# Cross attention with the state-space copy ahead of the exponential, and more places for expert weights

## The reference

```python
# block one
x = x + mixed @ w_out                    # convolution and dilated attention
x = x + memory_cross_attention(rms_norm(x), rms_norm(mem), w_xq, w_xk, w_xv, w_xo)
x = x + hierarchical_moe(rms_norm(x), ..., w1, w3, w2)        # stage one: 32 experts, ff 512
x = rms_norm(x)
# block two
x = x + mixed2 @ w_out_2                 # forgetting attention and a state-space layer
x = x + _hier_moe(rms_norm(x), ..., w_gate, w_up, w_down)     # stage two: 32 experts, ff 256
```

## Time and profile before

| | |
|---|---|
| median of 3 runs | 1988.65 us (1988.5 to 1989.75) |
| profiled execution, its own time | 1994.36 us |
| its span | 1992.5 us, 19337 instructions |
| TensorE busy | 1680.9 us (84%) |
| VectorE, ScalarE, GpSimd busy | 507.1, 332.1, 325.3 us |
| DMA | 437.02 MB, mean 219 GB/s |
| chain that ended last | TensorE 59%, DMA 28%, VectorE 5% |
| largest DMA parts of it | w1/w3/w2 into ring 17%, stage two's up weights into ring 10% |

### The profile page before, as it was taken

How to read it: one execution, slowest core, us unless ns; L and a number is a source line. 1 busy time by engine, 2 the same in 40 slices (tenths; PEclk the granted TensorE clock), 3 DMA queues, 4 the chain that set the end, 5 groups by cost and what they waited for, 6 DMA issues and landing times.

```text
span 1992.5 us, 19337 instructions
## 1 busy us (share of the span) xinstructions
PE 1680.9 (84%) x7362; PEld 846.6 (42%) x7362; DVE 507.1 (25%) x1204; ACT 332.1 (17%) x735; POOL 325.3 (16%) x325
## 2 busy tenths in 40 slices
PE   3999998899779787777777758899999997887775
PEld 2445776444444432322222224645744444543432
DVE  2466666120223320100000011622501015311110
ACT  2001552120222000000000021222510003011111
POOL 0011002956010111111111110011001010122212
PEclk9999999899899798999999988999999998899888
DMA  9112103420453599999999956761012235899994
GB/s 278 63 43 85 64 1 127 168 95 23 169 201 134 191 414 417 414 417 412 413 402 403 404 186 221 188 173 43 1 42 85 85 132 216 316 399 403 402 389 155
DMA packets 101675, 437.02 MB, mean 219 GB/s; under 512 B 15608, under 2 KB 23448, under 8 KB 75344
## 3 DMA queue, kind: packets, MB, share of 16 engines
q1 hardware_dynamic: 58320, 295.03, 38.9%
q10 hardware_dynamic: 24800, 109.99, 13.5%
q0 software_dynamic: 18464, 30.76, 6.1%
HBM read 414.19 MB, written 40.91 MB: 228 GB/s over the span
## 4 chain that ended last, share of the span: by engine, by line
PE 59%; DMA 28%; DVE 5%; ACT 2%; POOL 2%; issue 2%; SPq 1%; ACTq 0%; DVEq 0%; POOLq 0%
PE ps L245 28%; DMA ring<-in_w 17%; PE ps L1607 10%; DMA ring<-in_w_expert_up 10%; PE ps L1199 7%; PE ps L2078 2%; PE ps L1623 1%; PE ps L655 1%; PE ps L663 1%; DMA ring<-in_positions 1%; PE ps L2116 1%; PE ps L1225 1%; PE ps L452 1%; PE ps L2425 1%; PE ps L1008 1%
## 5 line engine op out<-in xcount | busy, mean ns | idle before, releaser
L1607 PE MATMUL ps<-ring,work 128*64 128x256 f32 (+1 forms) x2112 | 395.2, 532 | 118.4 <-DMA ring<-in_w 71.2
L1607 PEld LDWEIGHTS ps<-ring,work 128*64 128x64 f32 x2112 | 162.8, 151 | 357.3 <-issue 172.2
L245 PE MATMUL ps<-hT,ring 128*128 128x512 f32 x640 | 280.7, 598 | 2.5 <-DVE hT L1254 1.3
L1623 PE MATMUL ps<-ring,work 128*64 128x512 f32 x784 | 183.2, 601 | 38.3 <-issue 36.4
L245 PEld LDWEIGHTS ps<-hT,ring 128*128 128x128 f32 x640 | 122.2, 192 | 156.6 <-issue 154.0
L1725 DVE TENSOR_TENSOR work<-work,ps 128x256 f32<-128x256 f32 (+1 forms) x64 | 22.7, 355 | 644.5 <-ACT work L1684 625.4
L245 PE MATMUL ps<-ring,hT 128*128 128x512 f32 (+1 forms) x320 | 124.7, 550 | 0.3 <-PE ps L245 0.3
L1771 POOL DMA_INDIRECT hres<-work,rowdst x33 | 51.7, 1566 | 442.9 <-ACT work L1694 442.6
L245 PE MATMUL ps<-work,ring 128*128 128x128 f32 (+2 forms) x800 | 117.5, 293 | 1.7 <-DVEq L229 0.6
L1199 PE MATMUL ps<-ring,hT 128*128 128x512 f32 x256 | 112.9, 595 | 1.9 <-DVEq L229 0.9
L245 PEld LDWEIGHTS ps<-work,ring 128*128 128x128 f32 x800 | 105.6, 191 | 8.1 <-DVE ring L2482 2.3
(11 more groups left out here) (425 smaller groups left out, 1642.6 us busy)
## 6 DMA issues: line engine op xcount, KB each, us to landing
ring<-in_w SPq DMA_DIRECT2D x66, 2048.0 KB, 16.8
ring<-in_w ACTq DMA_DIRECT2D x30, 2048.0 KB, 20.5
ring<-in_w_expert_gate SPq DMA_DIRECT2D x34, 1024.0 KB, 19.9
ring<-in_w_expert_up SPq DMA_DIRECT2D x34, 1024.0 KB, 29.4
ring<-in_w_expert_down ACTq DMA_DIRECT2D x28, 1024.0 KB, 21.6
ring<-in_w_in SPq DMA_DIRECT2D x13, 2048.0 KB, 15.2
ring<-in_w_out SPq DMA_DIRECT2D x4, 2048.0 KB, 7.7
ring<-in_w_expert_down SPq DMA_DIRECT2D x6, 1024.0 KB, 14.4
```

The lines of the kernel that those rows point to most:

```text
L245: last = nc.tensor.matmul(out_, l, r, start=i == 0, stop=i == len(pairs) - 1)
L1607: last = nc.tensor.matmul(ps[64 * hf:64 * hf + 64, bank, 0:ff].rearrange("p (w n) -> p w n", w=2), xT[:, k, :], up[:, :, k * ff + hf * hw: ...
L1623: last = nc.tensor.matmul(ps[64 * hf:64 * hf + 64, bank, :], hT_[:, i % nch, 64 * (i // nch):64 * (i // nch) + 64], down[:, i, hf * 512:hf ...
```

## The change

In `xattn_act` the copy of state-space block i-1 is put ahead of the exponential of round i. The tiles `x`, `hT` and `xn` become three parts of one tile `kept`. A stage of experts may use it as a further place: a third in stage one (up weights over `hT` and `xn`, down weights over `x`), and two more in stage two, six in all. SP issues the loads for these places as soon as the first gathered block has landed (`xg6_0`), those that overwrite `x` also after its stores (`xinit6`). The planner's scratch moves from `hT` to the route area `RT` and to `junk`. Six more semaphores are used twice, which the tensor engine clears between the blocks. The calls of the stage functions pass 3 and 6 in place of 2 and 4, and the lag of the down products is told from `ff`, so it stays.

```diff
-        x = sb("x", [P, T, D])
-        hT = sb("hT", [P, KD, SEQ])
-        xn = sb("xn", [P, T, D])
+        kept = sb("kept", [P, 3 * T * D])
+        x = kept[:, 0:T * D].rearrange("p (t n) -> p t n", t=T)
+        hT = kept[:, T * D:2 * T * D].rearrange("p (k n) -> p k n", k=KD)
+        xn = kept[:, 2 * T * D:3 * T * D].rearrange("p (t n) -> p t n", t=T)
...
             for i in range(NX + 2):
+                if 1 <= i <= NX:
+                    s5_turned_act(act, i - 1)
                 if i < NX:
                     act.wait_ge(S("x5_max"), i + 1)
                     if i >= 2:
                         act.wait_ge(S("x5_turned"), since("x5_turned") + i - 1)
                     nc.scalar.activation(pr(i)[:, 0:MEM], ps[:, i % 2, 0:MEM], ACT.Exp, bias=nmax[:, i:i + 1], scale=-1.0,
                                          accum_out=den[:, i:i + 1]).then_inc(S("x5_probs"), 1)
-                if 1 <= i <= NX:
-                    s5_turned_act(act, i - 1)
...
-        late_rank = hl(256, T, NE)
-        egate = hl(384, 8, NE)
+        late_rank = hl(RT, 0, T, NE)
+        egate = hl(RT, 128, 8, NE)
...
-        Ab = hl(1672, 8, SLOT)
-        be_f = hl(2200, NOV, NE)
+        Ab = hl(junk, 0, 8, SLOT)
+        be_f = hl(junk, 512, NOV, NE)
...
-            if places == 2:
-                up, down = (ring[:, 0:2, :], ring[:, 2, :]) if e % 2 == 0 else (ring[:, 4:6, :], ring[:, 3, :])
+            place = e % places
+            if places == 3 and place < 2:
+                up, down = (ring[:, 4:6, :], ring[:, 3, :]) if place else (ring[:, 0:2, :], ring[:, 2, :])
             else:
...
+                size = 3 * KD * ff
+                in_ring = places * 2 // 3
+                if place < in_ring:
+                    at = (place + 2) % in_ring * size
+                    wv = ring[:, :, :].rearrange("p a n -> p (a n)")[:, at:at + size]
+                    up, down = wv[:, 0:2 * KD * ff], wv[:, 2 * KD * ff:size]
+                else:
+                    at = (places - 1 - place) * size
+                    up, down = kept[:, at + size - 2 * KD * ff:at + size], kept[:, at:at + size - 2 * KD * ff]
...
+            sp.wait_ge(S(f"xg{m}_0"), since(f"xg{m}_0") + 16)
+            for e in range(places * 2 // 3, places):
+                load_up(e)
+                if places == 3:
+                    sp.wait_ge(S(f"xinit{m}"), since(f"xinit{m}") + 16 * T)
+                load_down(e)
+                if e == 4:
+                    sp.wait_ge(S(f"xinit{m}"), since(f"xinit{m}") + 16 * T)
             for e in range(places, NE):
                 sp.wait_ge(S(f"up{m}"), since(f"up{m}") + e - places + 1)
                 load_up(e)
```

More of the change, by code:

```diff
@@ L133, in shared_semaphores @@
         shared[f"xg9_{q}"] = (f"xg6_{q}", 16 * NE // 2 // 4)
-    for i in range(4):
-        shared[f"w9_{i}"] = (f"w6_{i}", (16 if i % 2 else 32) * NE // 2)
+    for i in range(6):
+        shared[f"w9_{i}"] = (f"w6_{i}", (16 if i % 2 else 32) * len(range(i // 2, NE, 3)))
     for slot in range(RING):
@@ L1412, in slots_dve @@
                 dve.wait_ge(S(f"ranks{m}"), since(f"ranks{m}") + t1)
-                late = hl(0, T, 2, NE)
+                late = hl(junk, 0, T, 2, NE)
                 rank = (ps[:, 7, 0:3 * NE] if t0 == 0 else ps[:, 4, 0:NE]).rearrange("p (t e) -> p t e", t=n)
@@ L1450, in hl @@
             return v
-        late_rank = hl(256, T, NE)
-        egate = hl(384, 8, NE)
-        cnt = hl(640, 8, NE)
-        over = hl(896, NE, SEQ // SLOT - 1)
-        dests = hl(1120, 8, 4)
-        Gb = hl(1152, 8, NOV + 1)
-        Bb = hl(1288, 8, NOV)
-        Rb = hl(1416, 8, 2 * NOV)
-        Ab = hl(1672, 8, SLOT)
-        be_f = hl(2200, NOV, NE)
-        te = hl(2712, T, NE)
+        late_rank = hl(RT, 0, T, NE)
+        egate = hl(RT, 128, 8, NE)
+        cnt = hl(RT, 384, 8, NE)
+        Bb = hl(RT, 640, 8, NOV)
+        over = hl(RT, 1024, NE, SEQ // SLOT - 1)
+        Gb = hl(RT, 1248, 8, NOV + 1)
+        Rb = hl(RT, 1408, 8, 2 * NOV)
+        te = hl(RT, 1664, T, NE)
+        dests = hl(RT, 1792, 8, 4)
+        Ab = hl(junk, 0, 8, SLOT)
+        be_f = hl(junk, 512, NOV, NE)
         def late_dve(m, piece):
@@ L1507, in late_dve @@
                 L(dve.tensor_tensor(te, te, row("first_row").unsqueeze(1).to_broadcast(full), ALU.add))
-                pick = hl(0, T, 2, NE)
+                pick = hl(junk, 0, T, 2, NE)
                 L(dve.tensor_tensor(pick, E12[:, :, :, :], te.unsqueeze(2).to_broadcast([P, T, 2, NE]), ALU.mult))
@@ L1579, in expert_views @@
         def expert_views(ff, places, e):
[L1581 to L1588 removed]
+            place = e % places
+            if places == 3 and place < 2:
+                up, down = (ring[:, 4:6, :], ring[:, 3, :]) if place else (ring[:, 0:2, :], ring[:, 2, :])
+            else:
+                size = 3 * KD * ff
[7 more added lines that the diff above has]
+                    up, down = kept[:, at + size - 2 * KD * ff:at + size], kept[:, at:at + size - 2 * KD * ff]
+                up = up.rearrange("p (w n) -> p w n", w=2)
             return up, down.rearrange("p (c n) -> p c n", n=D)
@@ L1629, in moe_pe @@
         def moe_pe(pe, m, ff, places):
-            lag = 1 if places == 2 else 2
+            lag = 1 if ff == FF1 else 2
             n = lambda what, v: pe.wait_ge(S(f"{what}{m}"), since(f"{what}{m}") + v)
@@ L2610, in _ @@
             ranks_pe(6)
[L2611 to L2612 removed]
+            moe_pe(pe, 6, FF1, 3)
+            over_pe(pe, 6, FF1, 3)
             pe.wait_ge(S("pool_over"), 1)
@@ L2624, in _ @@
             ranks_pe(9)
-            moe_pe(pe, 9, FF2, 4)
-            over_pe(pe, 9, FF2, 4)
+            moe_pe(pe, 9, FF2, 6)
+            over_pe(pe, 9, FF2, 6)
         @block.scalar
```

31 lines of the change are left out of this document (12 added, 19 removed).

## The result

| | before | changed |
|---|---|---|
| median | 1988.58 us (1987.36 to 1989.75, 4 runs) | 1966.96 us (1964.34 to 1970.19, 4 runs) |
| ratio to before, 95% interval | | 0.9892 [0.9872, 0.9912] |
| profiled execution, its span | 1994.36, 1992.5 us | 1970.19, 1968.4 us |

The change gains 21.6 us, not 36, and the time lies 1 us above the range. The direction was right. The span of the profiled execution became 24.1 us shorter (these executions lie 5.8 and 3.2 us above the medians), and reading both traces at the same instructions splits these 24.1 us. Each column is the time from the event of the column before to this one, the first from the span's start; "up 31" are the up products of expert 31, "last down" the last down products of a stage, each by its start.

What follows compares the result with a forecast made beforehand. Transfers were taken to set 749 us of the expert stages, and ScalarE's copy to hold up TensorE in the cross attention. 14.5 + 10 + 11.5 = 36 us off the 1988.65 us median gave 1952.6 us, range 1942 to 1966.

Steps and rivals of the forecast that it cites:

- Cross attention, 14.5 forecast: Cross attention with ScalarE's copy ahead of the exponential: 2.8 + 8.4 + 3.3 = 14.5 us gained, bounds 9 and 21.8.
- The two groups of four rounds: Cross attention between value products: period 12.1 us in place of 16.3, 4.2 us gained, twice.
- the first piece: Start of the cross attention: copy 2 held until the first block store lands near 519.5 us; 2.8 us gained.
- nothing holds copy 2: Rival, cross attention: the first store lands before 514 us; 19.6 + 21.5 = 41 us gained, 1947.5 us; chance 0.10.
- Stage one, 10 forecast: Third place in stage one: 12.7 earlier start - 5.3 down transfer + 3.3 = 10.7, taken as 10 us; bounds 5 and 13.
- that lost 3.3 us, which a deeper queue fills: End of stage one: DMA share 0.62 over the last 8.65 us before the last up load landed; 3.3 us regained.
- Stage two, 11.5 forecast: Two more places in stage two: 9.0 + 3.8, less half the last down transfer, taken as 11.5 us; bounds 4 and 15.
- here all of it is paid back: Stage two: the 5.3 us of downs ahead of ups is regained, as the two overflow blocks' loads close the stream.
- the head start that goes into downs and isn't paid back: Rival, both expert stages: new places fill with downs first, TensorE late at the end; 23.5 us gained, 1965 us; chance 0.18.
- The stream itself runs slower: Rival, expert stages: a 4.8% lower rate over 749 us loses the 36 us; at 6%, 1998 us; chance 0.03.
- VectorE binds every round: Rival, cross attention: VectorE or the blocks' stores bind; 9 us there, total 30.5, 1958 us; chance 0.11.
- the new place does nothing: Rival, expert stages: the new place's loads wait as late as the first products; only cross attention counts, 1974 us; chance 0.03.

Runs made afterwards that it cites:

- late_first_load: The changed kernel, with SP issuing the first expert's up weights after the cross attention: 1959.41 us, ratio 0.9846; repeated in another set, 1952.92 us.
- down_late: The changed kernel, with down weights issued only two experts ahead in stage one and four in stage two, as before the change: 1968.26 us, ratio 0.9905.
- swap_only: The kernel before, with only ScalarE's copy of the state-space block put ahead of the exponential: 1977.17 us, ratio 0.9943.

## Why the prediction was wrong

**Cross attention, 14.5 forecast, 11.7 measured.** The two groups of four rounds gave 8.1 (forecast 8.4), the last piece 3.3 (3.3). The step that failed is the first piece, "1.8 us there and 1.0 in the fourth round: 2.8". It gave 0.3: the value products came at 529.10, and at 529.43 before. The mechanism was right, as late_first_load shows; three things were mis-sized. The store landed at 520.5 and not 519.5, since the issue 1.6 us earlier brought it nothing, and TensorE's clock stayed at half up to 526.4, because the engine stood still for 7.5 us. And the sum takes every round at full clock, where the kernel before had half of it from 512.1 to 524.8 us. That is luck of the execution: from the first scores to the first value products the traces with the old order take 23.0 us twice and, where the clock came back sooner, 20.8 twice, against 22.7 in the changed kernel. Measured by the shorter ones the first piece lost 1.9 us. In late_first_load the first value products begin 13.0 us after the first scores, in the changed kernel 22.7 us, so the hold and its clock cost 9.7 us; the rival "nothing holds copy 2" priced them at 5.1.

The Trainium skill ("DMA: Bandwidth & Descriptors", Queues, rings and completion order) says that each DMA engine goes round its queues a packet at a time. The traces agree in that the store had no right of way: in the kernel before it landed at 520.47 us and the load beside it at 520.29, and it took 10.0 us in the changed kernel and no store more than 5.8 with the load moved. That the small store ends only with the load, which the prediction drew from that rule, the page doesn't state; it is what these traces show.

**Stage one, 10 forecast, 7.0 measured.** The loads are issued 12.7 us earlier, and with the downs held back (down_late) the stretch shrinks by 12.7 against the kernel before and by 10.5 and 11.8 against the other two profiles with two places. The down transfer ahead of the ups cost 3.0 to 4.5 (forecast 5.3). What failed is "that lost 3.3 us, which a deeper queue fills": with the third place the share before the last landing is 0.36. A place more doesn't put work behind the last up weights, since the stage has no more to load (this reason is read from the program; the ten profiles with three places all have the low share). Another 1.2 went behind them, to the clock: the last up products took 9.94 us (8.78 in the earlier trace rows), and 7.09 in other runs.

**Stage two, 11.5 forecast, 2.4 measured.** Here the largest part is lost, and the step is "here all of it is paid back". I took the overflow blocks' loads for what closes the stage, because the queue had 3.8 us of empty time around them. But in the kernel before TensorE waits only 0.15 us for the last of them, in its timeline:

```profile
1964.24 3.67 PE L1607 MATMUL ps<-ring,work 128*64 128x256 f32 x32 [1.50 <-DVE work L1880]
1968.07 3.67 PE L1607 MATMUL ps<-ring,work 128*64 128x256 f32 x32 [0.15 <-DMA ring<-in_w_expert_up]
```

From expert 31's up products on, TensorE's own work sets the end there, so only their start counts, and it came 6.1 us sooner. With the downs held back it was 11.2: 9.0 of earlier start and 2.2 more, which I put down to the queue's empty time before expert 31's weights (a share of 0.78 over the 5.4 us before their landing in the kernel before); the missing 5.2 goes to the downs ahead of the ups and, as that run can't tell them apart, to SP's long issues (last section). This split is worked out and not tested by itself. The row with the wait of 0.15 us stands in the trace of the kernel before, and the prediction doesn't use it. Then came the wait for the gathered rows, which I had nowhere: the rows are gathered only after expert 28's result, and TensorE, which waits less for weights, now comes to them before the 9.2 us of the gather are over.

**The rival that held** is the head start that goes into downs and isn't paid back: stage one 5, stage two 4, 1965 us. It was given 0.18, and the row above and the fact that a stage can't fill its own end would have made it the likeliest. Its 1965 is near the 1966.96 partly by chance: the first piece of the cross attention is 2.5 lower than it has it, and the stretch between the stages gave 3.3 that belong to no part.

**Not foreseen:** the 3.3 us between the stages. Over the thirteen profiles that stretch has 521.5 to 522.6 us eight times and 525.0 to 525.6 five times, in one kernel both. In all five long ones the first 64 products take 9.77 to 9.91 us, in all eight short ones 7.13: that is 2.7 of the 3 to 4 us. The length comes by chance, and 3 to 4 us of it can stand in any difference between two profiles. The six further semaphores that TensorE clears there cost nothing that shows: swap_only, without them, took 521.75 us, the changed kernel 521.96 and 521.45. "The stream itself runs slower", "VectorE binds every round" and "the new place does nothing" are refuted by the rates, the 12.3 us and the 12.7 and 9.0 us.

## What to carry to other kernels

An earlier start of a stream that fills the engines is worth its time only as far as the transfers that end the stage move with it: ask what the new places fill with first, and read from TensorE's own waits at the stage's end whether a transfer or the engine's work closes it. Empty time in a queue is no gain if the row that waits for its last transfer waits 0.15 us. And when a copy is moved forward, the wait that held it for free (here a store beside a large load) must be priced with the clock that the idle engine loses; moving the load was worth 6.7 us in one set of runs, beside the 21.6 of the whole change (13 against the other set, of which 6.5 lie between two measurements of one kernel).

## What the hardware showed

- A 256 KB store took 10.0 us beside a 4.2 MB load on another queue, and 2.0 us with the load moved (the first store of late_first_load, and the median of its 16).
- After 7.5 us without work TensorE was granted half its clock (0.50 from 521.3 to 526.3 us, that is 1.2 GHz in place of 2.4), and the same products took 1.96 us in place of 1.09. In the kernel before it was granted half as well, from 512.1 to 524.8 us, with waits of 3.30 and 1.68 us. In late_first_load, with waits of 1.79 and 0.16 us, it kept 1.00. The moment at which the clock falls differs between executions of one kernel, and changes the time of 64 products from 7.13 to 9.8 us.
- With six places the issue of a load in stage two takes SP up to 9.9 us where none took more than 1.5 before, in SP's timeline below. The rates stayed as they were. In down_late, where the downs are only four ahead, no issue takes more than 2.1 us, so what that run gains up to expert 31 in stage two can't be told apart from these holds; stage one has no long issue, and there the downs alone cost 3.0 to 4.5 us.

```profile
1737.73 4.70 SPq L1793 DMA_DIRECT2D ring<-in_w_expert_up  x1
...
1769.23 9.91 SPq L1793 DMA_DIRECT2D ring<-in_w_expert_up  x1
```
